# Two-block network on one core: 64x64 tiles for attention's scores and turns, state products ahead of outputs in the recurrence

## What is computed

```python
# recurrence, per head and token
sa = einsum('bhvk,bhk->bhv', state, -kk_t)
state = state * w_t[:, :, None, :] + sa[..., None] * (kk_t * a_t)[:, :, None, :] + v_t[..., None] * k_t[:, :, None, :]
y = einsum('bhvk,bhk->bhv', state, r_t)
# attention, three patterns (window, stride) = (128, 1), (512, 4), (2048, 16), per head
s = einsum('bhgnqd,bhgnkd->bhgnqk', q, kb) / sqrt(hd), masked to the window
p = exp(s - max(s)); den = sum(p); o = einsum('bhgnqk,bhgnkd->bhgnqd', p, vb) / den
o = sum over patterns of softmax(lse) * o, then an RMS norm per head
x = x + concatenate([y_rwkv, y_attn]) @ w_out
```

## Time and profile before

| what | value |
|---|---|
| median of 3 executions | 3135.67 us (3131.33 to 3138.91) |
| the profiled execution's own time | 3130.07 us |
| its span, first to last instruction | 3128.2 us |
| TensorE busy | 3005.6 us, 96% of the span |
| VectorE, ScalarE busy | 1733.3 us (55%), 1236.0 us (40%) |
| granted TensorE clock, mean | 0.992 of full speed |
| the stage with attention | 1955 to 2330 us after the start |

### The profile page before, as it was taken

The page is one execution under the profiler, slowest core; times in us unless marked ns, Lnnn a source line. Parts: engine busy times, 40 slices in busy tenths (PEclk is TensorE's granted clock), DMA queues, the critical chain, the costliest instruction groups (busy, mean ns, idle before and its releaser), DMA issues.

```text
span 3128.2 us, 56034 instructions
## 1 busy us (share of the span) xinstructions
PE 3005.6 (96%) x23898; PEld 2484.5 (79%) x23898; DVE 1733.3 (55%) x3053; ACT 1236.0 (40%) x2133; POOL 160.1 (5%) x272
## 2 busy tenths in 40 slices
PE   8999999999999999999999999889889999999998
PEld 7898877889878888888777777667667778887886
DVE  7777643365773243435675554655646656666343
ACT  5334434333543221213453432555554434445332
POOL 1011000010000000000000000000002200000000
PEclk9999999999999999999999999999999999999999
DMA  4212132144322111112454422111013322224643
GB/s 147 82 64 94 59 121 82 52 139 156 118 98 74 54 43 59 38 52 86 136 178 157 135 92 96 60 30 33 26 67 130 122 86 83 81 81 154 193 125 121
DMA packets 102168, 297.59 MB, mean 95 GB/s; under 512 B 13296, under 2 KB 13424, under 8 KB 101792
## 3 DMA queue, kind: packets, MB, share of 16 engines
q1 hardware_dynamic: 83648, 237.34, 23.0%
q0 software_dynamic: 12944, 37.32, 3.4%
q10 hardware_dynamic: 5328, 19.34, 1.5%
HBM read 233.88 MB, written 57.94 MB: 93 GB/s over the span
## 4 chain that ended last, share of the span: by engine, by line
PE 80%; DVE 11%; ACT 6%; issue 2%; DMA 0%; POOL 0%; DVEq 0%; SPq 0%; ACTq 0%; POOLq 0%
PE ps L129 65%; PE ps L128 13%; DVE w_lo L168 1%; ACT w_hi L165 1%; PE ps L137 1%; DVE HB L168 1%; DVE HB L178 1%; DVE C L178 1%; DVE a_A L182 1%; ACT m_D L147 1%; DVE m_SS L178 0%; ACT L152 0%; DVE n L178 0%; DVE XLA L168 0%; ACT C L147 0%
## 5 line engine op out<-in xcount | busy, mean ns | idle before, releaser
L168 DVE TENSOR_TENSOR w_lo<-w_raw,w_hi 128x1024 fp32r<-128x1024 f32 (+3 forms) x354 | 373.8, 1056 | 395.9 <-ACT w_hi L165 394.4
L129 PE MATMUL ps<-XHA,w_hi 128*128 128x264 f32 (+3 forms) x1456 | 466.7, 321 | 10.5 <-DVE w_lo L168 5.3
L129 PE MATMUL ps<-XLA,w_hi 128*128 128x264 f32 (+3 forms) x1456 | 457.1, 314 | 0.0
L129 PE MATMUL ps<-XHA,w_lo 128*128 128x264 f32 (+3 forms) x1456 | 455.3, 313 | 0.0
L165 ACT ACTIVATE w_hi<-w_raw 128x1024 fp32r<-128x1024 f32 (+3 forms) x354 | 324.0, 915 | 293.0 <-PE ps L129 210.6
L129 PE MATMUL ps<-XHB,w_hi 128*128 128x512 f32 x920 | 368.0, 400 | 6.9 <-DVE w_lo L168 4.3
L129 PE MATMUL ps<-XLB,w_hi 128*128 128x512 f32 x920 | 358.9, 390 | 0.0
L129 PE MATMUL ps<-XHB,w_lo 128*128 128x512 f32 x920 | 358.8, 390 | 0.0
L129 PEld LDWEIGHTS ps<-XHA,w_hi 128*128 128x128 f32 x1456 | 275.6, 189 | 38.7 <-issue 13.6
L129 PEld LDWEIGHTS ps<-XLA,w_hi 128*128 128x128 f32 x1456 | 275.5, 189 | 21.2 <-issue 3.6
L129 PEld LDWEIGHTS ps<-XHA,w_lo 128*128 128x128 f32 x1456 | 276.0, 190 | 16.5
(11 more groups left out here) (448 smaller groups left out, 5587.8 us busy)
## 6 DMA issues: line engine op xcount, KB each, us to landing
w_raw<-in_f_gate SPq DMA_DIRECT2D x50, 512.0 KB, 3.3
w_raw<-in_f_up SPq DMA_DIRECT2D x50, 512.0 KB, 3.2
w_raw<-in_f_down SPq DMA_DIRECT2D x64, 384.0 KB, 3.2
w_raw<-in_w_out SPq DMA_DIRECT2D x32, 512.0 KB, 3.3
w_raw<-in_w_rkv SPq DMA_DIRECT2D x24, 512.0 KB, 3.4
w_raw<-in_w_attn SPq DMA_DIRECT2D x24, 512.0 KB, 4.1
h<-HB POOLq DMA_DIRECT2D x40, 256.0 KB, 2.5
hid<-C POOLq DMA_DIRECT2D x18, 512.0 KB, 2.9
```

Source lines behind the costliest of these rows:

```text
L129: return Issued(e.matmul(out, a, b, start=start, stop=stop))
L168: return Issued(self.eng and self.eng.tensor_tensor(out, a, b, op))
```

## The change

In attention, each `scores` call makes four products for two heads, each of 64 rows and 64 columns of weights, in place of two of 64 rows and 128 columns. The turns (of `aV` and of the weights) are no transposes: each block of 128x128 becomes four products of a 64x64 piece with a 64x64 identity, those of the upper 64 partitions into one bank, those of the lower into another (`quarters`). So a turn always takes two banks, one semaphore tells of the whole turn, and ScalarE's copies are two for each turn, one a bank, which write pieces of 64 columns with gaps of 64 (`by_side`). The warm-up products in front of round 0's `aV` are gone. In the recurrence, state product c is issued before the output product c-1; the first state product comes right behind `("KV")`, in its slot. VectorE loses a `yield` ahead of its four state steps and has one more behind. The last output product waits for VectorE's last state.

```diff
--- before.py
+++ after.py
@@ -2641,26 +2641,40 @@
         to_heads(b, 0, WU[:, :, 1, :], GB[:, :, 1, :], (), False)
         to_heads(b, 256, blk(x.Kt), blk(x.Vt), (), False)
         to_heads(b, 256, blk(x.Bt), WU[:, :, 1, :], (), False).then_inc(S.pe, ("KV", u))
-        yield
         FT, Rh = [a.rearrange("p (q g x) -> p q g x", q=2, x=64) for a in (x.FT, x.Rh)]
-        P.wait_ge(S.pe, ("KV", u))
-        P.wait_ge(S.dve, ("R", u))
-        for c in range(4):
-            q = c % 2
+        sides = lambda c: [(i, h, 2 * i + c // 2) for i in range(2) for h in range(2)]
+
+        def state(c):
+
             if u or c:
+                P.wait_ge(S.pe, ("KV", u))
+                P.wait_ge(S.dve, ("R", u))
                 P.wait_ge(S.dve, ("S", 4 * u + c))
-                sides = [(i, h, 2 * i + c // 2) for i in range(2) for h in range(2)]
-                for i, h, g in sides:
-                    op = P.mm(b[heads(h), q, 64 * g:64 * g + 64], x.state(u, c)[heads(h), i, :], Rh[heads(h), q, g, :], False, True,
-                              skip=True)
+                for i, h, g in sides(c):
+                    op = P.mm(b[heads(h), c % 2, 256 + 64 * g:320 + 64 * g], FT[heads(h), c % 2, g, :],
+                              x.state(u, c)[heads(h), i, :], False, True, skip=True)
+                op.then_inc(S.pe, ("S", u, c))
+
+        def output(c):
+
+            if u or c:
+                if u < 3 or c < 3:
+                    P.wait_ge(S.dve, ("S", 4 * u + c + 1))
+                for i, h, g in sides(c):
+                    op = P.mm(b[heads(h), c % 2, 64 * g:64 * g + 64], x.state(u, c)[heads(h), i, :], Rh[heads(h), c % 2, g, :],
+                              False, True, skip=True)
                 if c == 3:
                     op.then_inc(S.pe, ("YY", u))
-                if u < 3 or c < 3:
-                    for i, h, g in sides:
-                        op = P.mm(b[heads(h), q, 256 + 64 * g:320 + 64 * g], FT[heads(h), q, g, :], x.state(u, c)[heads(h), i, :],
-                                  False, True, skip=True)
-                    op.then_inc(S.pe, ("S", u, c))
+
+        state(0)
+        yield
+        for c in range(1, 4):
+            if u < 3 or c < 3:
+                state(c)
+            output(c - 1)
             yield
+        output(3)
+        yield
         sums("cen", 0, K.centre, x.yy, S.act, ("YY", u))
         yield
         sums("var", 1, K.ones64, x.sq, S.act, ("sq", u))
@@ -2854,7 +2867,7 @@
                     d, ("S", 4 * u + c + 1))
                 ps.done(("KV", u), (c % 2,), d, ("S", 4 * u + c + 1))
             yield
-        yield from pause(2)
+        yield from pause(3)
         V.wait_ge(S.act, ("rsd", u))
         for i, at in enumerate(ends):
             V.stt(x.yy[:, at], both[:, 0, at], vec("ln_w", i), x.rs[:, at], MUL, MUL).then_inc(d, ("cen", u))
@@ -2906,10 +2919,15 @@
 UNITS = [(i, h) for i in BLOCKS for h in range(2)]
 
 
+def by_side(a, side, n):
+
+    return a[:, :].rearrange("p (c s x) -> p s c x", s=2, x=64)[:, side, 0:n, :]
+
+
 def attention_load(D, K, j):
     S = K.at
     if j:
-        D.wait_ge(S.pe, ("v", j - 1, 4))
+        D.wait_ge(S.pe, ("v", j - 1))
     D.dma(K.aV[:, :], K.attn[8 + j]).then_inc(K.a_v, ("in", j), by=16)
     if j:
         D.wait_ge(S.pe, ("s", j - 1, 15, 512))
@@ -2929,16 +2947,21 @@
     S, ps = K.at, K.atb
     yield from pause(ATT)
     in3_over(P, K)
+
+    def quarters(banks, src, n):
+
+        for c in range(n):
+            for side, part in SIDES:
+                at = 128 * c + 64 * part
+                op = P.mm(banks[side][heads(part), block(c)], src[heads(side), at:at + 64], K.ident[heads(side), heads(side)], True,
+                          True)
+        return op
+
     for j in range(4):
         yield
-        for c in (0, 4):
-            b = ps.take(P, ("v", j, c))
-            if c == 0:
-                P.warm(b, K, f"v{j}")
-                P.wait_ge(K.a_v, ("in", j))
-            for n in range(4):
-                op = P.tp(b[:, 128 * n:128 * n + 128], K.aV[:, 128 * (c + n):128 * (c + n) + 128], K.ident)
-            op.then_inc(S.pe, ("v", j, c))
+        banks = [ps.take(P, ("v", j, h)) for h in range(2)]
+        P.wait_ge(K.a_v, ("in", j))
+        quarters(banks, K.aV, 8).then_inc(S.pe, ("v", j))
         P.wait_ge(K.a_ld, ("in", j))
         yield
 
@@ -2948,19 +2971,18 @@
             cn = min(512, 128 * (i + 1) - c0)
             if cn > 0:
                 banks = [ps.take(P, ("s", j, u + h, c0)) for h in range(2)]
-                for h in range(2):
-                    P.mm(banks[h][:, 0:cn], K.aq[heads(h), 128 * i:128 * i + 128], K.ak[heads(h), c0:c0 + cn], True,
-                         True).then_inc(S.pe, ("s", j, u + h, c0))
+                for part in range(2):
+                    for h in range(2):
+                        at = 128 * i + 64 * part
+                        op = P.mm(banks[h][heads(part), 0:cn], K.aq[heads(h), at:at + 64], K.ak[heads(h), c0:c0 + cn], True, True)
+                        if part:
+                            op.then_inc(S.pe, ("s", j, u + h, c0))
 
         def turn(u):
             i, h = UNITS[u]
             P.wait_ge(S.act, ("e", j, u))
-            for c0 in range(0, i + 1, 4):
-                b = ps.take(P, ("t", j, u, c0))
-                for c in range(min(4, i + 1 - c0)):
-                    op = P.tp(b[:, 128 * c:128 * c + 128], K.aA[h][:, 128 * (c0 + c):128 * (c0 + c) + 128], K.ident)
-                op.then_inc(S.pe, ("t", j, u, c0))
-            S.pe.at["t", j, u] = S.pe.n
+            banks = [ps.take(P, ("t", j, u, side)) for side in range(2)]
+            quarters(banks, K.aA[h], i + 1).then_inc(S.pe, ("t", j, u))
 
         def values(i):
             b = ps.take(P, ("w", j, i))
@@ -3015,10 +3037,10 @@
         yield
         if j:
             A.wait_ge(S.pe, ("w", j - 1, 7))
-        for c in (0, 4):
-            A.wait_ge(S.pe, ("v", j, c))
-            A.cp(K.aVT[:, 128 * c:128 * c + 512], ps["v", j, c][:, :]).then_inc(a, ("VT", j))
-            ps.done(("v", j, c), a, ("VT", j))
+        A.wait_ge(S.pe, ("v", j))
+        for h in range(2):
+            A.cp(by_side(K.aVT, h, 8), by64(ps["v", j, h][:, :])).then_inc(a, ("VT", j))
+            ps.done(("v", j, h), a, ("VT", j))
         yield
 
         def weights(u):
@@ -3033,11 +3055,10 @@
             i, h = UNITS[u]
             if i:
                 A.wait_ge(S.pe, ("w", j, i - 1))
-            for c0 in range(0, i + 1, 4):
-                cn = min(4, i + 1 - c0)
-                A.wait_ge(S.pe, ("t", j, u, c0))
-                A.cp(K.aPT[h][:, 128 * c0:128 * (c0 + cn)], ps["t", j, u, c0][:, 0:128 * cn]).then_inc(a, ("p", j, u))
-                ps.done(("t", j, u, c0), a, ("p", j, u))
+            A.wait_ge(S.pe, ("t", j, u))
+            for side in range(2):
+                A.cp(by_side(K.aPT[h], side, i + 1), by64(ps["t", j, u, side][:, 0:64 * (i + 1)])).then_inc(a, ("p", j, u))
+                ps.done(("t", j, u, side), a, ("p", j, u))
 
         def values(i):
             A.wait_ge(S.pe, ("w", j, i))
```

## The result

The changed kernel takes 3146.81 us (median of 8, 3144.15 to 3150.41), the kernel before beside it 3134.72 us. The ratio is 1.0039, 95% interval 1.003 to 1.0048: 12 us slower. The forecast was 3125.5, and the range ended at 3138. The profiled execution has a span of 3145.3 us against 3128.2. By the timeline, the first turn of `aV` begins at 1960.1 us (1958.3 before), so 1.8 us of the 17.1 are there ahead of it; the next projection's first product begins at 2348.0 (2331.9 before), 16.1 us later. The loss is inside the stage that was meant to gain.

The account below looks back on a forecast made before the run. The stage was taken as mostly, not wholly, bound by TensorE's work in fixed order. Terms: -13.5 + 2 + 0.5 + 0.3 + 1.5 - 0.5 = -9.7 us; from the runs' median 3126.0, stated as 3125.5, range 3110 to 3138.

Parts of the forecast that it names:

- 8 x 14.6 = 0.117 us: Price on TensorE of one transposed block as eight instructions at 14.6 ns; 320 blocks make 37.4 us.
- Turns: Transposes on TensorE, taken as 44.5 us now, become 37.4 us plus 1.6: gain 5.5 us (1 to 9).
- Scores: Attention's score products on TensorE, on four tiles: 32.5 us against about 41 by starts, gain 9 us (7 to 12).
- Shape changes: TensorE leaves and re-enters 64x64 tiles 40 times less each, at 0.10 and 0.05 us: gain 6 us (3 to 9).
- Conversion: Of 20.5 us of TensorE work saved in the stage, two thirds count on the chain: 13.5 us.
- Clock: Without the warm-up products TensorE idles nearly all of 1956 to 1961.9; one more low-clock stretch costs 1.5 us (0 to 3).
- Recurrence: State products ahead of output products come 0.25 us sooner, but the wait's cause remains: net -0.5 us (-3 to +2).
- ScalarE: Copies cost 0.17 us an instruction plus 0.83 ns a column; extra and later copies make 11.4 us, a fifth counts: +2.
- C: Rival, chance 0.06: in the four small blocks of each round, scores wait for ScalarE's copies through the bank ring; +16, 3142.
- D: Rival, chance 0.04: tiles don't run side by side in a turn, 0.24 us a block, +26 on the chain: 3152.
- milder form: From the Trainium skill: starts never closer than about 25 ns, so 0.2 us a block, 64 us for all turns: about 3143.
- chance of a faster kernel: Faster by over 0.2%: TensorE's savings counting in full or all state waits gone (0.25), plus nine tenths of the forecast's 0.45: 0.67.

## Why the prediction was wrong

**The step that failed is "8 x 14.6 = 0.117 us" for a turned block, multiplied by 320.** The 14.6 ns were read rightly and hold after the change. What failed is the use of a short group's pace for a stage that would have 4831 instructions more. The stage's late starts rose from 5.2 to 18.4 us. The prediction had "POOL and SP issue nothing new" and no term for TensorE's own instruction queue, though the page showed it and the earlier trace rows is from the view that lists "issue". The turns, which were to gain 5.5 us, lost 13.5.

*Turns.* Of the 13.5 us, about 4.7 are the second bank's and 8.5 are more late starts (13.7 - 5.2). The gain of 5.5 us was never there. By starts, and without the idle time that the profile counts, the 288 transposes of the weights took 41.4 us and as products, alone, 46.0. The 32 blocks of `aV` took 4.1 and 4.2. So all 320 transposes took 45.5 us, near the 44.5 that I took, and as products they took 50.2 in place of 39.0. Of the 46.0, 33 us are at the pace, and 13 us are 93 starts over 70 ns. 48 of these lie inside turns, 5.9 us: most are the first step of a group (0.109 in place of 0.058 us), and some end at a wait. The other 45 lie at the step to other work, 7.4 us, and 21 of them are the same 0.148 us ahead of a call of scores, whose tile has another shape in this run. This fits the cost of leaving 64x64, which the changed kernel doesn't pay there. The three counts overlap and add up to more than 13.5, so the split is not shown to the microsecond.

*Scores.* The price of a call for 512 keys was right, 0.87 to 0.91 us against the 0.9 taken. By starts, all scores took 41.3 us before, the "about 41" of the prediction, but 36.9 in scores alone and not 32.5. What was priced too low is the rest: with what stands ahead of the next group, the calls for 384, 256 and 128 keys took 0.77, 0.65 and 0.38 us, where 0.68, 0.45 and 0.23 were taken, and all 24 for 512 took 0.95 on average. The gain by starts was 4.4 us and not 9. In the time it is 4 us.

*Shape changes.* TensorE leaves 64x64 tiles 79 times before (1955 to 2330 us) and 46 times after (1955 to 2348), and comes back 78 and 45 times. That is 33 fewer of each, where I had 40. No run has this term alone.

*Conversion.* Two thirds of the saved work was to count. Scores alone have 4 of 4.4 us, with an interval from 0 to 7.5, so they neither confirm nor refute it.

*Clock.* One more low stretch was forecast, 3.4 us long and 1.5 us dear. It was 17 us long. Where the earlier trace rows had the warm-up, the engine did this:

```profile
1960.05 1.98 PE L129 MATMUL ps<-cst,a_V 64*64 64x64 f32 x64 [2.13 <-DMA a_V<-attn]
1963.57 1.13 PE L128 MATMUL ps<-r_GK,r_in 64*64 64x64 f32 x32 [1.53 <-DMA a_k<-attn]
```

2.13 and 1.53 us idle, with the turn of `aV` between, at a clock of 0.50 to 0.69 by the windows. It is worth 3 us by the medians and 4 by the mean clocks, about the upper bound given, and not settled.

*Recurrence.* Forecast -0.5 (-3 to +2); measured -1 with an interval from -4 to +2. Within the forecast, and the reason given fits: the waits for `r_S` stayed at 6.3 and 6.7 us.

*ScalarE.* The copies' formula held: one of 64 columns took 222 ns in the trace after (0.17 + 0.05 = 0.22), and the one signal cost nothing measurable.

*The parts together.* Turns +13.5, scores -4, recurrence -1, and 3 for the missing warm-up make about 12, which was measured.

*Rivals.* C was the nearest, with 0.06: right mechanism, 5 us of the 16. D named the right quantity, the time between starts in turns, and looked for its cause in the tiles. Its milder form, 3143, came out closest to the measured time, but by luck: 24 instructions of a turn still took 14.6 ns each after the change. The chance of a faster kernel was added up wrongly: its parts make 0.655 and not 0.67.

Scores alone, at 0.9988 (0.9976 to 0.9999), is the fastest kernel here, if by little; with the recurrence's order added the gain could not be told from none.

## What to carry to other kernels

Count instructions as well as columns when one product is cut into small ones. Ask how long the densest run of them is, not only what one costs: here a group of 128 ran at a pace that the instruction queue could not follow over 1024. A hole in the middle of a group, with "issue" as its releaser and at the same number modulo 256 as the others, was the mark of it. And a helper that takes two banks in place of one is a change of every wait around the ring; price it alone.

## What the runs showed of the hardware

- On this chip TensorE's instructions came in transfers of 16 KB, and in a burst of 64x64 products of 64 columns the 256 instructions of one ran in 1.9 us and a stop of 1.4 us followed: at best 256 instructions in 3.48 us. After a stop the engine went on 2.2 to 2.9 us after a transfer had begun.
- A block turned by two products with 64 rows and 128 columns of weights took 0.23 us, twice the 0.117 of four products on 64x64 tiles, though it is half the instructions.
- With five products of 128x256 left out ahead of a wait for a DMA, TensorE stood at 1.2 GHz for 17 us, with 8.4 us busy in the ten from 1966 on; with them put back, for 3.4 us there.
- The trace with them put back has a stretch of 13.7 us at 1.2 GHz at the end of the stage (from 2338 us), which the trace without them lacks. One execution does not tell where the low level comes.
